# Input fetched transposed, two weight slices in native fp32, and 512-column matmuls for every expert tile of ten turns

## The reference, cut to what matters

```
h = rms_norm(x, norm1_g)
proj = h @ w_in                  # 1024 x 2816: S5 input ua, then q, k, v, and the retention parts
ya, yb, yc = s5(ua), moba(q, k, v), retention(...)
x = x + (concat(ya, yb, yc) * mix_out_g) @ w_out
h2 = rms_norm(x, norm2_g)
q = h2 @ peer_w_q;  sc = scores of q against sub_keys      # PEER: 16,384 experts
top 16 of 128 twice, then 16 of 256, softmax  ->  expert numbers and gates of each token and head
x = x + sum over chosen experts of gate * gelu(h2 . u_emb[e]) * v_emb[e]
```

## Time and profile before

| | us |
|---|---|
| median of 3 runs (901.4 to 901.64) | 901.53 |
| the profiled execution, its own time | 901.37 |
| its span in the trace | 899.6 |
| PE busy | 891.8 (99%) |
| DVE busy | 744.5 (83%) |
| ACT busy | 576.9 (64%) |
| POOL busy | 426.4 (47%) |

### The profile page before, as it was taken

One profiled execution on the slowest core, in us unless ns is written; L12 is line 12 of the kernel. 1 busy time (PEld: TensorE's weight loads), 2 busy tenths in 40 slices (PEclk: granted clock), 3 DMA queues, 4 the chain that ended last, 5 costly groups with the idle time before them and its releaser, 6 DMA issues.

```text
span 899.6 us, 18356 instructions
## 1 busy us (share of the span) xinstructions
PE 891.8 (99%) x4842; PEld 761.1 (85%) x4842; DVE 744.5 (83%) x1697; ACT 576.9 (64%) x1182; POOL 426.4 (47%) x342
## 2 busy tenths in 40 slices
PE   8999999999999999999999999999999999999998
PEld 5877888899999888888888888888888888888886
DVE  7979535199999859999999988888888888888886
ACT  7759566665555567777777776565656565655563
POOL 5875288889999987777777772000000000000000
PEclk9999999999999999999999999999999999999999
DMA  9835050566666665555565657766667677666663
GB/s 335 296 108 188 1 211 23 197 204 231 232 233 231 229 221 207 202 199 209 189 219 186 216 184 262 246 236 235 244 243 244 238 243 244 233 240 247 242 239 128
DMA packets 67755, 191.52 MB, mean 213 GB/s; under 512 B 6672, under 2 KB 8592, under 8 KB 67728
## 3 DMA queue, kind: packets, MB, share of 16 engines
q1 hardware_dynamic: 67440, 191.09, 60.6%
q10 hardware_dynamic: 288, 0.10, 0.0%
HBM read 173.86 MB, written 17.30 MB: 212 GB/s over the span
## 4 chain that ended last, share of the span: by engine, by line
PE 94%; DVE 3%; DMA 1%; ACT 0%; SPq 0%; issue 0%; DVEq 0%
PE ps L763 24%; PE ps L450 16%; PE ps L451 16%; PE ps L452 16%; PE ps L765 11%; PE ps L773 3%; PE ps L717 2%; PE ps L762 2%; DMA routing<-in_w_in 1%; DVE ps L836 1%; PE ps L719 1%; DVE routing L836 1%; DVE ps L1014 1%; PE ps L736 0%; PE ps L611 0%; PE ps L442 0%
## 5 line engine op out<-in xcount | busy, mean ns | idle before, releaser
L1673 ACT ACTIVATE w_hi<-raw 128x512 fp32r<-128x512 f32 x512 | 308.2, 628 | 136.1 <-PE ps L452 135.3
L1840 POOL TENSOR_TENSOR w_lo<-raw,w_hi 128x512 fp32r<-128x512 f32 x256 | 327.1, 1300 | 67.2 <-ACT w_hi L1673 66.4
L763 PE MATMUL ps<-h_both,w_hi 128*128 128x512 f32 x936 | 331.5, 394 | 0.0
L765 PE MATMUL ps<-h_both,w_lo 128*128 128x256 f32 x819 | 229.4, 280 | 0.0
L836 DVE TENSOR_TENSOR w_lo<-raw,w_hi 128x512 fp32r<-128x512 f32 x256 | 177.3, 693 | 57.1 <-ACT w_hi L1673 41.8
L763 PEld LDWEIGHTS ps<-h_both,w_hi 128*128 128x128 f32 x936 | 173.8, 188 | 31.1 <-issue 0.2
L450 PE MATMUL ps<-w_hi,hot_gate 128*128 128x512 f32 x512 | 199.2, 389 | 0.0
L452 PE MATMUL ps<-w_hi,hot_gate 128*128 128x512 f32 x512 | 199.2, 389 | 0.0
L451 PE MATMUL ps<-w_lo,hot_gate 128*128 128x512 f32 x512 | 199.2, 389 | 0.0
L765 PEld LDWEIGHTS ps<-h_both,w_lo 128*128 128x128 f32 x819 | 154.7, 189 | 1.1
L1720 ACT ACTIVATE con<-ps 128x256 f32<-128x256 f32 x117 | 45.0, 385 | 108.4 <-PE ps L763 108.4
(11 more groups left out here) (242 smaller groups left out, 1090.2 us busy)
## 6 DMA issues: line engine op xcount, KB each, us to landing
raw<-in_u_t SPq DMA_DIRECT2D x128, 512.0 KB, 4.0
raw<-in_v SPq DMA_DIRECT2D x128, 512.0 KB, 3.3
act_spill<-acts SPq DMA_DIRECT2D x62, 256.0 KB, 2.2
acts<-act_spill SPq DMA_DIRECT2D x62, 256.0 KB, 3.4
routing<-in_w_in SPq DMA_DIRECT2D x4, 2048.0 KB, 11.9
routing<-in_w_out SPq DMA_DIRECT2D x2, 2048.0 KB, 7.6
routing<-in_w_q SPq DMA_DIRECT2D x2, 2048.0 KB, 7.7
routing<-in_w_in SPq DMA_DIRECT2D x2, 1024.0 KB, 10.7
```

The lines of the kernel that those rows point to most:

```text
L763: mm = pe.matmul(ps[:, s % 2, :], s_hi, both, start=(h == 0 and k == 0), stop=end)
L765: mm = pe.matmul(ps[:, s % 2, 0:S], s_lo, m_hi, start=False, stop=False)
L1673: A.activation(w_hi[:, 2 * (s % 2) + h, :], raw[:, s, h * HALF:(h + 1) * HALF], ACT.Copy)\
L1840: G.tensor_tensor(w_lo[:, slot, :], raw[:, s, h * HALF:(h + 1) * HALF], w_hi[:, slot, :].bitcast(F32), ALU.subtract).then_inc(lo_ready, 1)
```

## The change

1. **Input.** The host passes x transposed as well (`x_t`), and the S5 columns of `w_in` laid out by partition (`w_u`). SP fetches four pieces of two chunks of each, in turn (256 KB a piece). PE's sixteen transposes and their wait for the identity are gone; a third matmul on zeros is added. x itself is fetched later, ahead of block 6's wait, for the residual sum.
2. **Scaling and sum of squares.** ACT scales chunks 0 to 3 from SBUF, POOL chunks 4 to 7 (they were DVE's). ACT squares the transposed x in four parts, DVE adds the parts up, and PE sums over partitions with two matmuls of one column.
3. **Native slices.** The first two slices of block 1 are multiplied in native fp32 (`native_slices`, four matmuls of 512 columns) straight from `hT` and the weights; their high and low parts are made no more, and every count of slices made falls by NATIVE = 2. The small S5 steps follow later slices: the transposes of u behind slice 3, those of B behind slice 4, `drive(0)` behind slice 5, `drive(1)` behind slice 5 of block 2. The low parts of chunks 0 and 1 of the input are needed from block 2 on only; DVE makes them behind `bb`.
4. **DVE's order.** The three small products `rope_k` move from before `states(0)` to behind `states(1)`.
5. **Experts.** In turns 2 to 11 all four tiles are wide. Ten more copies on ACT and ten more adds on DVE come in, and `PART_STEPS` is written anew with 46 places instead of 36.

```diff
+NATIVE = 2
...
-WIDE_S, WIDE_SEL, WIDE_LAST = (0, 1, 2, 3), (0, 1, 2), (0, 1, 2)
+WIDE_LAST = (0, 1, 2)
...
-WIDE_TURNS = {0: 0, 1: 4, **{t: 8 + 3 * (t - SEL0) for t in range(SEL0, SEL1)}}
-WIDE_TURNS |= {t: 8 + 3 * (SEL1 - SEL0) + UN * (t - SEL1) for t in range(SEL1, G_TURN0)}
+WIDE_TURNS = {t: UN * t for t in range(G_TURN0)}
...
-PART_STEPS = (21, 30, 39, 62, 71, 80, 89, 95, 101, 115, 121, 126, 129, 130, 131, 135, 147, 156, 176, 185, 197, 215, 216, 223,
-              236, 242, 249, 260, 261, 262, 264, 265, 266, 271, 276, 281)
+SEL_PARTS = [(t, s) for t in range(SEL0, ROUTE_TURN) for s in range(UN)]
+
+PART_STEPS = (21, 31, 40, 49, 61, 71, 80, 83, 88, 95, 101, 107, 114, 120, 127, 128, 129, 130, 131, 132, 134, 146, 156, 165,
+              175, 184, 197, 206, 214, 216, 222, 228, 235, 241, 248, 254, 258, 261, 262, 263, 264, 265, 266, 272, 277, 282)
...
+        xT = rot_tmp.rearrange("p (k t) -> p k t", k=KC)
...
-            for t in range(TT):
-                sp.dma_start(xs[:, t, :], x[t * P:(t + 1) * P, :]).then_inc(x_in[t], 16)
-            first = w_src[0].rearrange("(k p) n -> p k n", p=P)
-            sp.dma_start(w_ring[0][:, 0:4, 0:S5_CH], first[:, 0:4]).then_inc(first_in, 16)
-            sp.dma_start(w_ring[0][:, 4:KC, 0:S5_CH], first[:, 4:KC]).then_inc(w_in_sem[0], 16)
+            for i in range(4):
+                ks = slice(2 * i, 2 * i + 2)
+                sp.dma_start(xT[:, ks], x_t[:, ks]).then_inc(x_t_in[i], 16)
+                sp.dma_start(w_ring[0][:, ks, 0:S5_CH], w_u[:, ks]).then_inc(first_in[i] if i < 3 else w_in_sem[0], 16)
...
+                    if n == 6:
+                        for t in range(TT):
+                            sp.dma_start(xs[:, t, :], x[t * P:(t + 1) * P, :]).then_inc(x_in[t], 16)
...
-            for _ in range(2):
+            for _ in range(3):
                 pe.matmul(ps[:, 7, :], mv[:, 0, 0:P], mv[:, 0, :], start=True, stop=True)
-            pe.wait_ge(con_in, 16)
-            transpose_rows(xs, x_in)
             for k in range(KC):
-                if k == 0:
-                    pe.wait_ge(first_in, 16)
-                if k == 4:
-                    pe.wait_ge(w_in_sem[0], 16)
-                pe.wait_ge(full_act if k < 4 else full_dve, k % 4 + 1)
+                if k % 2 == 0:
+                    pe.wait_ge(first_in[k // 2] if k < 6 else w_in_sem[0], 16)
+                pe.wait_ge(full_act if k < 4 else full_pool, k % 4 + 1)
...
+            pe.wait_ge(zeros_ready, 6)
+            pe.wait_ge(ss_ready, 1)
+            for t in range(TT):
+                mm = pe.matmul(ps[:, 5, t:t + 1], x_ss[:, t * P:(t + 1) * P], ones, start=True, stop=True)
+            mm.then_inc(ss_psum, 1)
+
+            def native_slices(ks):
+
+                pe.wait_ge(second_in, 16)
+                for k in ks:
+                    for t in range(TT):
+                        mm = pe.matmul(ps[:, t, :], hT[:, k, t * P:(t + 1) * P], w_ring[1][:, k, :], start=(k == 0), stop=False)
+                    mm.then_inc(half_used, 1)
...
+                        pe.wait_ge(th_pool if k in (4, 5) else th_ready, k - 3 if k in (4, 5) else k - 1)
+                        pe.wait_ge(tl_ready, k - 1)
+                    if k == 0 and n == 2:
+                        pe.wait_ge(tl_first, 2)
...
-            by_slices(1, range(0, 1))
+            native_slices(range(NATIVE))
+            by_slices(1, range(2, 4))
+            pe.wait_ge(con_in, 16)
...
-            by_slices(1, range(1, 2))
+            by_slices(1, range(4, 5))
...
-            by_slices(1, range(2, 3))
+            by_slices(1, range(5, 6))
...
-            by_slices(1, range(3, KC))
-            by_slices(2, range(0, 4))
+            by_slices(1, range(6, KC))
+            by_slices(2, range(0, 6))
             pe.wait_ge(turn_ready, S5_C)
             drive(1)
-            by_slices(2, range(4, KC))
+            by_slices(2, range(6, KC))
...
-                keys_turn(t, wide=WIDE_SEL)
+                keys_turn(t, wide=range(UN))
...
-            dve.wait_ge(sumsq_x, TT)
-            for k in range(4, KC):
-                dve.wait_ge(t_psum, k // 2 + 1)
-                V.tensor_scalar(hT[:, k, :], ps[:, k // 2, (k % 2) * S:(k % 2 + 1) * S], cols(V_G1 + k, 1), None,
-                                ALU.mult).then_inc(full_dve, 1)
-            dve.wait_ge(full_dve, 4)
+            sq_p = ps[:, 2, :]
+            for i in (1, 2):
+                dve.wait_ge(sq_x, i + 1)
+                step(tt(sq_p, sq_p, x_sq[:, i], ALU.add))
+            dve.wait_ge(sq_x, 4)
+            did(tt(x_part, sq_p[:, 0:S], x_sq[:, 3, 0:S], ALU.add))
+            did(tt(sq_p[:, S:2 * S], sq_p[:, S:2 * S], x_sq[:, 3, S:2 * S], ALU.add))
+            settle()
+            tt(x_ss, sq_p[:, S:2 * S], x_part, ALU.add).then_inc(ss_ready, 1)
+            dve.wait_ge(ss_ready, 1)
...
+                rstd_of(1, 0, TT, rx[:, 0:TT]).then_inc(rx_ready, 1)
...
-            rstd_of(1, 0, TT, rx[:, 0:TT]).then_inc(rx_ready, 1)
-            for k in (4, 5):
-                dve.wait_ge(th_ready, k + 1)
-                tt(h_lo[:, k, :], hT[:, k, :], h_hi[:, k, :].bitcast(F32), ALU.subtract).then_inc(tl_first, 1)
...
+            for k in range(2):
+                dve.wait_ge(th_ready, k + 3)
+                tt(h_lo[:, k, :], hT[:, k, :], h_hi[:, k, :].bitcast(F32), ALU.subtract).then_inc(tl_first, 1)
...
+                    dve.wait_ge(x_in[t], 16)
...
+            act.wait_ge(zeros_ready, 5)
+            A.activation(spare, quarter, ACT.Exp)
             act.wait_ge(params_in, 16)
             for k in range(4):
                 full(k)
-            rounded(range(0, 6))
-            act.wait_ge(zeros_ready, 5)
-            act.wait_ge(sumsq_x, TT)
-            root(ss_x, 0, 1.0 / D)
-            slices_high(range(0, 1))
-            act.wait_ge(ang_ready, 1)
-            did(A.activation(s1, ang, ACT.Sin))
-            settle()
-            A.activation(c1, half, ACT.Sin).then_inc(trig_ready, 1)
-            slices_high(range(1, 2))
+                if k == 1:
+                    squares_x(0)
+                    act.wait_ge(expo_ready, 1)
+                    A.activation(mag, expo, ACT.Exp).then_inc(mag_ready, 1)
+            squares_x(1)
+            squares_x(2)
+            rounded((2, 3))
+            squares_x(3)
+            rounded((0, 1))
+            A.activation(spare, quarter, ACT.Sqrt)
+            slices_high(range(2, 3))
+            act.wait_ge(ss_psum, 1)
+            root(ps[:, 5, 0:TT], 0, 1.0 / D)
+            slices_high(range(3, 4))
...
+            act.wait_ge(ang_ready, 1)
+            did(A.activation(s1, ang, ACT.Sin))
+            settle()
+            A.activation(c1, half, ACT.Sin).then_inc(trig_ready, 1)
+            rounded((6, 7))
+            slices_high(range(4, 5))
...
-                keys_turn(t, wide=WIDE_SEL, wide_0=3 * t + (WIDE_TURNS[SEL0] - 3 * SEL0))
+                keys_turn(t, wide=range(UN), wide_0=UN * t, carried=UN * t)
...
-            for k in range(4):
-                pool.wait_ge(th_ready, k + 1)
+            pool.wait_ge(params_in, 16)
+            for k in range(4, KC):
+                pool.wait_ge(x_t_in[k // 2], 16)
+                G.tensor_tensor(hT[:, k, :], xT[:, k, :], cols(V_G1 + k, 1).to_broadcast([P, S]), ALU.mult).then_inc(full_pool, 1)
+
+            def input_halves(k):
+
+                pool.wait_ge(full_pool, k - 3)
+                G.tensor_copy(h_hi[:, k, :], hT[:, k, :]).then_inc(th_pool, 1)
+                pool.wait_ge(th_pool, k - 3)
                 input_low(k)
-            slices_low(range(0, 1))
+
+            for k in (2, 3):
+                pool.wait_ge(th_ready, k - 1)
+                input_low(k)
+            input_halves(4)
+            slices_low(range(2, 4))
+            input_halves(5)
+            slices_low(range(4, 6))
             for k in (6, 7):
-                pool.wait_ge(full_dve, k - 3)
-                G.tensor_copy(h_hi[:, k, :], hT[:, k, :]).then_inc(th_pool, 1)
-                pool.wait_ge(th_pool, k - 5)
+                pool.wait_ge(th_ready, k - 1)
                 input_low(k)
-                slices_low(range(k - 5, k - 4))
-            slices_low(range(3, 33))
+                slices_low(range(k, k + 1))
+            slices_low(range(8, 33))
```

120 lines of the change are left out of this document (52 added, 68 removed).

## The result

The changed kernel takes 904.02 us (median of 12 runs, 902.44 to 904.34) against 901.26 for the kernel before (12 runs beside it). The ratio is 1.0029, 95% interval [1.0022, 1.0037]: **2.8 us slower**, where 2.7 faster was forecast. The profiled execution took 903.77, its span is 901.9 (before 899.6).

What follows compares the result with a forecast made beforehand. PE was taken to bound the kernel (busy 891.8 of 899.6 us). The front's 2.0 and the experts' 0.7 made 2.7 off the profiled 901.37, 898.7, or 898.8 for the median; range 897.3 to 900.9.

Steps and rivals of the forecast that it cites:

- The native matmul: Block 1's first two slices: a native fp32 matmul of 512 columns costs 0.85 us, four of them 3.4.
- Rival (d): At the start, PE's clock falls to 1.2 GHz through waits for pieces, ending 10 us later at 908.8; chance 0.04.
- The price of a wide tile: Expert turns 2 to 11: wide tiles instead of narrow ones gain 0.6 to 1.2 us over ten turns, 0.7 taken.
- The front's 2.0: From the start to slice 24: 2.1 us of PE's earlier start pass through, taken as 2.0.
- So `second_in` lands at 13.6 as before: Block 1's first weights: same bytes ahead of them, so they land at 13.6 us and native slices start then.
- Rival (a): Block 1's weights: landing goes by issue, not bytes, slips 1.8 us, front gives 0.2, end 900.6; chance 0.10.
- The moved `rope_k` adds 0.78: DVE between `states(0)` and `head_sums(1)`: the three products add 0.78 us that hid in idle time before.
- rival (b): DVE or ACT later by a microsecond or more, passing in full to slice 24; at one, 899.8; chance 0.09.
- behind slice 24 everything moves together: After slice 24 both lists are unchanged, so the same 2.0 us distance should hold to the first expert tile.
- So the total fits with 3 us to spare.: Expert turns: ten more DVE adds cost 3.4 us, against 4.9 of waits and a lead of 1.6.
- Rival (c): Expert turns: adds after step 261 come late, PE and ACT lose about 1 us, widening gives nothing, 899.8; chance 0.06.
- The chance of 0.06 for "slower": Whole kernel: 0.06 that it measures slower, against 0.69 faster and 0.25 the same; bounds 899.7 and 903.3 us.

Runs made afterwards that it cites:

- the mended front: Changed kernel's front, experts part undone, `rope_k` in its old place, input and S5 columns in unbroken pieces: 900.17 us, ratio 0.9991; also inside later kernels.
- e10_pad: `e9_both` with four tiny ACT copies added at its start: 899.58 us, ratio 0.9978 to the kernel before.
- after: The changed kernel itself, as profiled against the kernel before: median 904.02 us, ratio 1.0029.
- e2_front: Changed kernel with its experts part undone, so the front alone: 902.13 us, ratio 1.0010 to the kernel before.
- e13_late: `e9_both` with the three `rope_k` multiplications behind the second states again: 900.91 us, ratio 0.9992 to the kernel before.
- e11_after: Changed kernel with only the selection's two small integer results moved to PSUM: 901.59 us, ratio 0.9999 to the kernel before.
- e9_both: Changed kernel with `rope_k` in its old place, unbroken input and S5 pieces, and the two integer results in PSUM: 899.54 us, ratio 0.9977.

## Why the prediction was wrong, step by step

**Right.** What bounds the kernel, and that a change pays by PE's start or by PE's content. The native matmul: twice the projection's price, 0.85 forecast, 0.78 measured (3.13 for four). Rival (d) did not come: 0.78 for 512 columns is less than twice the projection's 0.424 for 256, while the matmuls on zeros, of the same form, took some 1.8 each in this profile too ((6.75 - 1.46) / 3). The granted clock reads 1.00 in both stretches and can't tell them apart, so the prediction's account of the start by the clock stays an inference. The price of a wide tile: 0.5 to 0.7 gained over ten turns where DVE let it (0.7 forecast). So what bounds PE was read well, and three costs were missed. The front's 2.0 was not right even so: with both of its faults mended it gives 1.4 at the y matmuls and 1.0 at the experts. The landing is then still 0.4 behind the 13.6 that the sum used. From the y matmuls to the second tile of turn 2 the mended front takes 95.2, the old one 94.8, where the sum took no loss; ACT's stall above may be a part of it (95.06 in `e10_pad`, without it), which no run shows for certain.

**"So `second_in` lands at 13.6 as before", since the bytes are the same.** It landed at 14.80. The step took the rate of the earlier trace rows for a property of the queue, but it belonged to those transfers: in 2 to 13 us the old front moves 351 to 360 GB/s, the changed one 295 to 311. The changed pieces are 128 rows of 2 KB at a distance of 8 KB. In unbroken runs (321 to 335 GB/s) the same bytes came 0.85 earlier on the mean, about half of the way back to the old front's 13.16. Rival (a) had a slip of 1.8 (chance 0.10) where 1.2 came, and the wrong mechanism: with the issue 2.4 us earlier nothing landed earlier. PE's own list was late too: the projection ended at 14.0, not 12.9, since the zeros' matmuls ended at 6.75 and pieces came late. Why these pieces move slowly is open. Broken rows alone are not the reason: the kernel before fetched the S5 columns straight from `w_in`, as rows of 1 KB at a distance of 11 KB, inside the 339 to 377 GB/s of 4 to 10 us. No run told the distance of the rows from their length, or either from the number of pieces.

**"The moved `rope_k` adds 0.78".** It added 2.60. The price was read from a row whose surroundings went unread: the earlier trace rows has it at 21.45, POOL's running pair ended at 22.01, so 0.78 already held a wait, hidden in idle time. At the new place POOL runs without a gap and the wait is on the path, 2.60 to 2.62 in three of the four profiles (`after`, `e2_front`, `e13_late`), 1.47 in `e11_after`, where the first one starts before a subtraction's end and not behind it. That DVE's 1.8 would pass on was said in the prediction ("each one passes in full to slice 24"); its rival (b) gave this kind of delay 0.09, at one microsecond. The step "behind slice 24 everything moves together" fell with it: the rotation of k, on DVE, was late too, and PE waited for it at 60.84.

**"So the total fits with 3 us to spare."** The ten adds cost what was said (3.4): DVE's busy time in 180 to 330 us went from 134.50 to 138.13 in the experts part alone, and from 132.65 to 136.38 with the results in PSUM. What failed is the reserve. The earlier trace rows gave 4.9 us of waits and the earlier trace rows 1.6 of lead, and the sum treated them as one stock. But idle time in one part of the stretch can't pay for lateness in another: in 183 to 312 us of the changed kernel 1.5 of waits before adds are left over, while DVE ends 2.3 late. In the late part, in the changed kernel, seven instructions of the selection (a subtraction, the shifts, an and, and the casts, L1293 to L1305) wait for POOL by 0.5 to 1.1 each, two in the first half and five in the second. Rival (c) named the place (adds behind step 261) and priced it at nothing gained, 899.8; it was 1.6 lost. The waits for POOL were in the trace of before as well, as in this integer shift of 128x128 (0.21 to 0.28 where it does not wait), and my count of DVE's steps took them for the instruction's own price:

```profile
222.73 1.31 DVE L1289 TENSOR_SCALAR routing<-routing 128x128 uint32<-128x128 uint32 x1
```

The chance of 0.06 for "slower" was too low mostly because losses on DVE, though named, were priced one at a time and small. Both parts put more work on the engine whose durations depend on its neighbour.

## What to carry to other kernels

A duration read from a row holds only with the neighbours it had: before an instruction is moved, look at what the engines it shares something with do at the old place and at the new one, and take the shortest row of the same shape as its own price. Idle time of an engine is a reserve only for work that comes ahead of it in the same stretch. The same bytes in another layout and other pieces are another transfer; one profile's start of a stage is one sample, and a gain of a microsecond wants several; and a buffer moved to PSUM can be worth more than the rearrangement it stands beside.

## What the runs showed of the hardware

**DVE waits for GpSimd's running instruction.** In the changed kernel the three `rope_k` multiplications (two operands from SBUF) take 0.36 where POOL is idle and 2.60 beside POOL's back-to-back subtractions, and the shift and cast from SBUF to SBUF take 1.24 and 1.3 instead of 0.28 and 0.42 with one side in PSUM; ends fall together with POOL's within 0.2 us. FIND_INDEX8 and MAX8 over 256 elements keep their 0.42 and 0.41 beside the same POOL instructions. The Trainium skill (SBUF — State Buffer, SBUF: two separate sides) says that DVE and GpSimd share a pair of ports under an exclusive lock, held for a whole instruction, which a DVE instruction takes when it runs in a two-port mode, or has two SBUF inputs while GpSimd's reads SBUF (as these subtractions do). The rows named here agree, and so does the wait of 1.47 in `e11_after`. It was the page that spoke against the move of `rope_k`, and the prediction did not use it.

**The DMA rate went with the layout and the pieces**: four pieces of 2 KB rows moved 161 to 240 GB/s at 6 to 8 us (DMA engines busy for 0.78 to 0.92 of it), two of 4 KB rows 319, four unbroken ones 303 to 352 (0.96 to 1.01), and the old front, 1 KB rows of `w_in` among it, 362 to 372; in 2 to 4 us everything with rows 8 KB apart moved 186 to 221, the unbroken pieces 262 to 276 and the old front 269 to 307. In 4 to 6 us the unbroken pieces are the slower ones (220 against 327), so the landing, not one window, is what to compare.

**A stall of 0.3 us tied to a place in ACT's stream**, behind a wait: the copy starts 0.36 behind PE's last matmul in `e9_both` and 0.10 behind it in `e10_pad`, with four instructions put in far ahead. What causes it is open.
